# Parity tiles for the dilated attention, four strips for the modulation sums, and two slots weighed alone

## The reference

```python
A_PATTERNS = ((128, 1), (512, 4), (2048, 16))        # window, dilation, one group of 8 heads each
def hybrid_layer(x, mod, ...):
    shift, scale, gate = split(mod)                  # mod = silu(c) @ w_ada + b_ada
    h = rms_norm(x, norm_g) * (1 + scale) + shift
    a_qkv, a_z, m_cq, m_ckv, m_kr, m_z, merge = split(h @ w_in)
    y_a = dilated_mixer(a_qkv, rel_bias) * silu(a_z)
    y_m = mla_mixer(...) * silu(m_z)                 # latent attention, 16 heads
    g_a, g_m = split(sigmoid(merge))
    return x + gate * ((g_a * (y_a @ w_out_a) + g_m * (y_m @ w_out_b)) @ w_o)
```

## Time and profile before

| | |
|---|---|
| median of 3 runs | 2422.16 us (2420.01 to 2424.64) |
| the profiled execution | 2423.71 us |
| its span | 2421.9 us |
| instructions | 28489 |
| PE busy | 1964.8 us (81%) |
| DVE, ACT, POOL busy | 56%, 29%, 25% |
| moved by DMA | 744.49 MB, mean 307 GB/s |

### The profile page before, as it was taken

The page is one execution under the profiler, slowest core; times in us unless marked ns, Lnnn a source line. Parts: engine busy times, 40 slices in busy tenths (PEclk is TensorE's granted clock), DMA queues, the critical chain, the costliest instruction groups (busy, mean ns, idle before and its releaser), DMA issues.

```text
span 2421.9 us, 28489 instructions
## 1 busy us (share of the span) xinstructions
PE 1964.8 (81%) x10561; PEld 1127.1 (47%) x10561; DVE 1357.4 (56%) x3340; ACT 713.2 (29%) x2013; POOL 610.5 (25%) x531
## 2 busy tenths in 40 slices
PE   8997878556867866877776656659999999999998
PEld 6654444111532421442431111115877884787786
DVE  5657856767777467687577876442433422004433
ACT  1222422333262323353333333220014320003430
POOL 0002433454334334334344444430000000000000
PEclk9998998777998887899887686789999999999999
DMA  8547999999999999999999999986752343532322
GB/s 302 212 127 299 401 406 416 419 421 421 419 419 406 415 418 416 419 418 410 419 418 418 406 422 417 414 363 229 282 195 62 105 140 110 206 134 78 132 99 83
DMA packets 199351, 744.49 MB, mean 307 GB/s; under 512 B 42326, under 2 KB 55662, under 8 KB 133672
## 3 DMA queue, kind: packets, MB, share of 16 engines
q0 software_dynamic: 73728, 536.90, 53.8%
q1 hardware_dynamic: 112500, 201.82, 23.5%
q10 hardware_dynamic: 12984, 3.94, 0.7%
HBM read 741.49 MB, written 1.12 MB: 307 GB/s over the span
## 4 chain that ended last, share of the span: by engine, by line
PE 42%; DMA 37%; DVE 9%; ACT 4%; issue 3%; PEld 3%; POOL 1%; PEldq 0%; DVEq 0%; SPq 0%; ACTq 0%; POOLq 0%
DMA expert_rows<-in_peer_uv,expert_ids 35%; PE psum L326 12%; PE psum L3387 6%; PE psum L2164 5%; DVE expert_rows L2264 4%; PE psum L2848 3%; PEld psum L3140 3%; PE psum L3403 2%; PE psum L1848 2%; ACT coefs_on_diagonal L2581 1%; PE psum L3212 1%; PE psum L3434 1%; PE psum L2013 1%; PE psum L3034 1%; PE psum L3421 1%
## 5 line engine op out<-in xcount | busy, mean ns | idle before, releaser
L2164 PE MATMUL psum<-expert_rows,coefs_on_diagonal 64*64 64x512 f32 x4096 | 682.6, 779 | 420.8 <-ACT coefs_on_diagonal L2581 420.4
L2264 DVE SCALAR_TENSOR_TENSOR expert_rows<-expert_rows,x 128x1024 f32<-128x1024 f32 x512 | 627.1, 1225 | 412.6 <-DMA expert_rows<-in_peer_uv,expert_ids 409.3
L2744 POOL DMA_INDIRECT expert_rows<-in_peer_uv,expert_ids x512 | 604.0, 1180 | 1001.8 <-PE psum L2164 752.5
L2164 PEld LDWEIGHTS psum<-expert_rows,coefs_on_diagonal 64*64 64x64 f32 x4096 | 149.2, 160 | 812.0 <-ACT coefs_on_diagonal L2581 602.7
L2571 ACT ACTIVATE gelu_dots<-dots 128x2 f32<-128x2 f32 x256 | 52.1, 204 | 881.8 <-DVE expert_rows L2264 881.6
L326 PE MATMUL psum<-xT,ring 128*128 128x256 f32 (+1 forms) x1264 | 277.9, 381 | 2.3 <-DMA ring<-in_mlstm_w_in 2.3
L326 PEld LDWEIGHTS psum<-xT,ring 128*128 128x128 f32 (+1 forms) x1264 | 238.0, 189 | 42.1 <-issue 9.8
L2581 ACT ACTIVATE coefs_on_diagonal<-ident,coefs 128x128 f32<-128x128 f32 x512 | 177.5, 393 | 8.3
L1848 PEld LDWEIGHTS psum<-xT,ring 128*128 128x128 f32 (+1 forms) x1088 | 129.3, 183 | 78.4 <-issue 78.4
L3059 POOL COPY ring<-ring 128x512 f32<-128x512 f32 x2 | 1.2, 614 | 587.9 <-DMA ring<-in_w_uq 587.9
L1848 PE MATMUL psum<-xT,ring 128*128 128x128 f32 (+1 forms) x1088 | 148.7, 287 | 0.0
(11 more groups left out here) (440 smaller groups left out, 2030.4 us busy)
## 6 DMA issues: line engine op xcount, KB each, us to landing
ring<-in_w_in SPq DMA_DIRECT2D x64, 1024.0 KB, 7.3
ring<-in_peer_w_q SPq DMA_DIRECT2D x24, 1024.0 KB, 19.0
first_modulation_weights<-in_w_ada SPq DMA_DIRECT2D x12, 1024.0 KB, 7.3
ring<-in_w_out SPq DMA_DIRECT2D x12, 1024.0 KB, 12.4
ring<-in_w_ada SPq DMA_DIRECT2D x12, 1024.0 KB, 6.5
expert_rows<-in_peer_uv,expert_ids POOLq DMA_INDIRECT x512, 16.3
ring<-in_rglru_w_in SPq DMA_DIRECT2D x8, 1024.0 KB, 21.1
ring<-in_w_out_b SPq DMA_DIRECT2D x8, 1024.0 KB, 6.3
```

Of the source, the lines that this page charges most:

```text
L2164: last = pe.matmul(psum[64 * half:64 * half + 64, 2 * t + m, :], diag[tokens, n % DIAGS, tokens], rows[tokens, at_, D + half * 512:D + (ha ...
L2264: dve.scalar_tensor_tensor(out=rows[:, at_, 0:D], in0=rows[:, at_, 0:D], scalar=1.0, in1=x[:, n // TILE % NT, :], op0=ALU.mult, op1=ALU.mu ...
L2744: pool_.indirect_dma_start(out=rows[:, n % ROWS, :], out_offset=None, in_=table, in_offset=bass.IndirectOffsetOnAxis(ap=ids[:, at_:at_ + 1 ...
```

## The change

- Queries and the keys of groups 1 and 2 (dilations 4 and 16) are written to the chip with even tokens first and odd tokens behind (`copy_parity`); the keys of group 0 stay in token order. A query tile is now the even or the odd tokens. It sees all 256 keys of group 0 and the 128 keys of its own parity in groups 1 and 2: 512 columns a head for both tiles.
- The values of groups 1 and 2 are dealt to even and odd by four transfers from chip memory to chip memory (64 partitions x 4 KB each), which ACT issues behind the reading of `rc`; PE waits for them ahead of the first `weighted`.
- The bias tiles are loaded in six transfers, in pieces of 512 bytes, and issued behind the loads of `rc`, ahead of those of `rmz`.
- Scores have two banks a head, used in turn, so that they wait for the maxima of the step before the last; the transposes have one bank a head, the attention's output bank 6; `shared` is gone.
- `Modulation` reduces by four products into four strips of 32 partitions, DVE adds four times 128.
- The last two slots of the stream are weighed singly, and the hold of the second block's first loads is given up after slot 505 in place of slot 508.

```diff
-            for half in range(2):
-                if n >= RING:
+            if n >= RING:
+                for half in range(2):
                     pe.wait_ge(bank_read[n % RING][half].sem, n // RING)
-                pe.matmul(bank(n % RING, half)[0:1, 0:256], ones[:, 0:1], self.acc[:, g % 2, half * 256:half * 256 + 256],
-                          start=True, stop=True).then_inc(half_done[half].sem, 1)
+            for part in range(4):
+                last = pe.matmul(self.sums(n, part), ones[:, 0:1], self.acc[:, g % 2, part * P:(part + 1) * P],
+                                 start=True, stop=True)
...
+        def sums(self, n, part):
+            return bank(n % RING, part // 2)[32 * part:32 * part + 1, 0:P]
...
+        def tiles_in(col, offset, step):
+            src = bass.AP(scr.tensor, offset, [[step, P], [DA_G * SPAN, DA_H], [1, P]])
+            sp.dma_start(bias[:, :, col:col + P], src).then_inc(skew_sem.sem, 16)
...
+                elif n == slots - 1:
+                    pe.wait_ge(coefs.sem, c0 + slots // PAIR + 1)
...
-                weigh(p)
+                if n < slots - PAIR:
+                    weigh(n, PAIR)
+                else:
+                    weigh(n, 1)
+                    weigh(n + 1, 1)
...
-        weights.hold = (added.sem, ad0 + slots - 3)
+        weights.hold = (added.sem, ad0 + slots - 6)
...
-        if layer == 0:
-            weights.small_loads = keep.pop("bias_rows")
         rz = weights.add([(w, 0, P, KD)], 4608, 512, 1)
...
         rc = weights.add([(w, 0, P, KD)], 5120, 416, 1)
+        if layer == 0:
+            weights.small_loads = keep.pop("bias_rows")
         rmz = weights.add([(w, 0, P, KD)], 5536, 512, 1)
...
+        def copy_parity(copy, dst, b):
+            return copy(dst.rearrange("p a (e i) -> p a e i", e=2), b.rearrange("p (a i e) -> p a e i", a=2, e=2))
...
+            for c in range(NT):
+                for e in range(2):
+                    act.dma_start(dealt[64 * c:64 * c + 64, e, :], vt[e:P:2, c, DA_W:DA_G * DA_W])\
+                        .then_inc(values_dealt.sem, 16)
             s1(act)
...
-        fill = (0, 2, 3, 4, 5, 6, 7, 1)
+        fill = (0, 1, 2, 3, 4, 5, 7, 6)
...
+            own = slice(t * P, (t + 1) * P)
+            return [(0, 0, slice(0, T)), (1, T, own), (2, T + P, own)] if t == 0 else [(1, 0, own), (2, P, own), (0, T, slice(0, T))]
...
+            first = 2 * i + step % 2 if dilated else 2 * i
+            return psum[:, first, 0:width(tile_of(step))]
...
+            return psum[:, 4 + (i if dilated else 2 * i), 0:width(tile_of(step))]
+        out = psum[:, 6, 0:T] if dilated else psum[:, 1, 256:512]
+        spare = 1 if dilated else 0
...
-                if step:
-                    pe.wait_ge(biased.sem, b0 + step)
+                if step > spare:
+                    pe.wait_ge(biased.sem, b0 + step - spare)
...
+                elif values_at:
+                    pe.wait_ge(*values_at)
```

More of the change, by code:

```diff
@@ L2577, in weigh @@
                 if s >= DIAGS:
-                    act.wait_ge(added.sem, ad0 + s + PAIR - DIAGS)
-                for q in range(PAIR):
+                    act.wait_ge(added.sem, ad0 + s + count - DIAGS)
+                for q in range(count):
                     ins = act.activation(diag[:, (s + q) % DIAGS, :], ident[:, :], ACT.Copy,
@@ L2811, in second_layer @@
         if layer == 0:
-            place[0] = ya_end + 8 * 1024
+            place[0] = ya_end + 2 * 1024
             mod = Modulation(1)
+            assert place[0] <= at_phase + 72 * 1024
             place[0] = attend_at
@@ L2896, in scalar @@
             read_both(act, rz, lambda g, half, b: act.activation(az[:, 2 * half:2 * half + 2, :], two(b), ACT.Silu))
-            for run, dst, first in rqk:
-                read_out(act, 0, run, lambda g, b: act.copy(dst[:, first:first + 2, :], two(b)))
+            for i, (run, dst, first) in enumerate(rqk):
+                read_out(act, 0, run, lambda g, b: copy_parity(act.copy, dst[:, first:first + 2, :], b) if dealt_in(i)
+                         else act.copy(dst[:, first:first + 2, :], two(b)))
             if mod:
@@ L2901, in scalar @@
             read_both(act, rc, lambda g, t, b: act.copy(lat[:, t, :], b[:, 0:416]))
+            n = rv_.first + rv_.count - 1
+            for half in range(2):
+                act.wait_ge(bank_read[n % RING][half].sem, n // RING + 1)
+            for c in range(NT):
+                for e in range(2):
+                    act.dma_start(dealt[64 * c:64 * c + 64, e, :], vt[e:P:2, c, DA_W:DA_G * DA_W])\
+                        .then_inc(values_dealt.sem, 16)
             s1(act)
@@ L2969, in bias_of, with da_value @@
         def bias_of(p, t):
-            both = [by_group(bias[:, 2 * p + i, :])[:, :, 0:(t + 1) * P] for i in range(2)]
-            return [b[:, :, ::-1] for b in both]
+            return [bias[:, 2 * p + i, t * T:t * T + 512].rearrange("p (b k) -> p b k", b=4)[:, :, ::-1] for i in range(2)]
+        def da_value(p, i, g, c):
+            first = (2 * p + i) * DA_D
+            if g:
+                return dealt[:, c, (g - 1) * DA_W + first:(g - 1) * DA_W + first + DA_D]
+            return vt[:, c, first:first + DA_D]
         rmz_last = weights.add([(w, 0, P, KD)], 6048, 512, 1)
@@ L3314, in second_layer, with pair_attention @@
             stage(tensor=tensor, vector=vector, scalar=scalar)
-    def pair_attention(n, queries, keys, values, groups, scale, bias_of, z, y, beside=(), then=None):
+    def pair_attention(n, queries, keys, values, groups, scale, bias_of, z, y, beside=(), then=None, values_at=None):
         steps, G = 2 * n, groups
@@ L3414, in turn @@
                 flat = probs[t][i].rearrange("p g k -> p (g k)")
-                blocks = list(range(G * (t + 1)))
-                shared = blocks[:2] if len(blocks) > 4 and i else []
-                for b in [b for b in blocks if b not in shared] + shared:
-                    if shared and b == shared[0]:
-                        pe.wait_ge(copied.sem, c0 + 2 * step + 1)
-                    last = pe.transpose(bank_t(step, i)[:, b * P:(b + 1) * P], flat[:, b * P:(b + 1) * P], ident[:, :])
+                for b in range(width(t) // P):
+                    at_ = home(t, b)
+                    last = pe.transpose(bank_t(step, i)[:, at_ * P:(at_ + 1) * P], flat[:, b * P:(b + 1) * P], ident[:, :])
                 last.then_inc(turned.sem, 1)
```

112 lines of the change are left out of this document (70 added, 42 removed).

## The result

The changed kernel takes 2406.1 us (median of five runs, 2401.8 to 2410.8), the kernel before 2422.2 (five runs beside them, 2418.6 to 2425.0). The ratio is 0.9940, with a 95% interval of 0.9928 to 0.9953, which is 11.4 to 17.4 us less. The forecast was 2406.0. The profiled execution took 2410.8 us, the longest of the five, and has a span of 2409.0. Three executions far above the others of their kernel (3196.8 and 5026.5 us of the variant attention_alone, 3207.8 of the kernel before) are left out of every median and ratio given here.

The account below looks back on a forecast made before the run. PE's timeline was taken to bound the kernel (PE 42% of the span, DMA 37%). Terms -11.3 + 0 + 0 - 3.0 - 1.45 = -15.8 us gave 2406 from a median of 2422.2, range 2403 to 2409.

Parts of the forecast that it names:

- Attention: Dilated attention, two layers: fewer score columns, transposes and waits save 5.55 us in layer 0 and 5.75 in layer 1, -11.3.
- rival C: Stream's end and layer 1's attention: gathers don't suffer (-2.4) and the low clock goes (-1.7); total -19.9, 2402 us; 12%.
- Dealing: Values dealt by four ACT transfers: 2.5 us of issues fit the room and the 1 MB is hidden; 0, bound +2.
- Bias tiles: Bias loads between `rc` and `rmz`: 10.7 us at 28 ns a piece, `rmz` 3.3 us ahead of need; 0.
- Rival D: Late `rmz`: 512 B bias pieces cost as much as 1 KB ones; +4, 2410 us; 8%.
- E: Slower than before: bias pieces cost as 2 KB ones, PE stands 18.6 us for `rmz`; total +2.8, 2425 us; 4%.
- Strips: Modulation sums: four strips take 0.40 us in place of 1.02, six times, one saving lost, DVE's additions hidden; -3.0.
- The stream's end: Last slots and first loads: single weighing and earlier hold release, slots stretched to 3.24 us, first product at 1630.6; -1.45.
- Rival A: Stream's end: gathers keep only half the slow engine, a slot takes 4.96 us; +4.6 there, total -9.7, 2412 us; 10%.

Follow-up runs that it names:

- attention_alone: Changed kernel with modulation sums, pairs of slots and hold as before; attention, dealing and bias tiles kept: 2409.8 us, ratio 0.9949.
- wait_back: Changed kernel with the removed wait put back: the second head's turns wait after two blocks for ACT's copy of the first head: 2410.1 us.
- bias_twice: Changed kernel with the six bias tile loads made twice, the second set behind the landing of the first, ahead of `rmz`: 2423.8 us.
- bias_twice_deal_late: As bias_twice, but the four dealt transfers are issued behind ACT's reading of `rmz`: 2421.1 us.
- warm_hold4: As warm, but the hold on the second block's first loads is given up after slot 507 in place of 505: 2405.0 us, ratio 0.9923.
- bias_first: Changed kernel with DVE adding the bias of a sum ahead of its multiplication for the next sum: 2405.6 us, ratio 0.9929.
- hold_late: Changed kernel with the hold given up after slot 508, the last two slots still weighed singly: 2411.1 us.
- warm: bias_first plus three needless PE products ahead of each of the last groups of slots, over the last 16 slots: 2404.9 us, ratio 0.9934.

## Why the prediction was right, and where its steps were not

The time was met (2406.1 against 2406.0), with one term too small, one too large, and one half eaten by the clock. That it was met to a tenth is luck: the five runs lie 9 us apart, and the errors of the terms partly cancel.

- **Attention, -11.3 forecast, -12.5 measured.** Layer 0 came as worked out: -5.4 against -5.55. Scores 1.15 forecast and measured; a pair 13.25 and 13.24; the two last weighted products 3.0 us forecast, 1858.66 - 1855.45 = 3.2 measured. The weighted product took 1.89 where 1.93 to 1.96 was put. wait_back shows the wait that was forecast: 0.68 a pair and 2.7 a layer hung on it. Layer 1 gave 1.3 more than its term, because the low clock of its last product went; the prediction had left it in, with its going as -1.7 of rival C. It is gone in all twelve profiles with the new attention; what made it go isn't shown, as layer 0's product had the same gaps ahead of it and ran at the full clock.
- **Dealing, 0 forecast, 0 measured.** The four issues took 2.48 us (2.5 forecast). The stretch up to the attention is 16.43 us in both kernels. But the step said of the 1 MB only that it had time, not that it cost others any: bias_twice and bias_twice_deal_late show 6.2 us of the engines' time taken from the weights when these are late.
- **Bias tiles, 0 forecast, 0 measured.** 293 GB/s were measured, and 28 ns a piece give the same. The room was smaller than the 3.3 us forecast: in warm_hold4, where everything ahead is 1 to 2 us shorter and SP issues `rmz` at 1771.53, PE waits 0.21 us for it at 1784.32, 12.8 us behind the issue. With the same 12.8 us the changed kernel's `rmz`, issued at 1775.72, would be there at 1788.5, 1.7 us ahead of need, an estimate. The forecast had SP issue at once; SP took 11.08 us to issue the six transfers of bias tiles and came to `rmz` only then. Rival D (+4) and E (slower) didn't come. The Trainium skill, "DMA: Bandwidth & Descriptors", "Specifications", names 512 B as the least that still goes at the line's rate; here 293 GB/s stand against 387 with 2 KB pieces, so at 512 B the rate was a quarter lower. The bias tiles' pieces also start at skewed addresses, a few bytes further for each partition, and no run separates this from their size.
- **Strips, -3.0 forecast, -1.5 measured. This is the step that failed.** The sentence "DVE's four additions in place of two are hidden" is wrong. DVE adds the bias of a sum behind its multiplication for the next, and that addition gives back the bank that PE's next product needs. With shorter sums PE is there sooner, and the additions take 1.18 us for four in place of 0.74 for two: PE waits 0.8 us in three places. Also the wait on the load of `w_ada`, which the forecast charged at 0.7, grew by 1.2. bias_first removes the first and is 2.84 below before, 2.3 to 2.8 below the three profiles with the old sums.
- **The stream's end, -1.45 forecast, -2.2 measured at the first product, -0.5 at the transposes of tile 1.** The shared slot was put at 3.24 us; the dots came 3.11 and 3.27 apart. Rival A (4.96 us a slot) is refuted. But the prediction misread the rule that it named. The Trainium skill, "DMA: Bandwidth & Descriptors", "Queues, rings and completion order", says that an engine goes round the queues packet by packet; it doesn't say that the turns are equally long. The trace of before shows turns equal in number: from 300 to 330 us, where the weight queue moved 1338 pieces in 23.5% of the time, the gathers' queue has this row:

```profile
q0 software_dynamic: 1338, 9.74, 78.5%
```

Both queues moved as many pieces, one of at most 8 KB for each one of 2 KB, so the time goes by the size of the pieces. It also prices the slot: its 128 rows are eight on each of sixteen engines, and eight turns of 85 ns for the weights add 0.68 us to 2.48, 3.16 by this estimate. The product began 0.8 us ahead of forecast. The forecast had the hold given up at -0.3 from the dot of slot 507 and 3.6 slots stretched, 2.7 us in all; PE made slot 505 at the low clock (3.69 us for the pair, not 1.95), SP issued only at +1.55, and two slots were stretched, by 1.4 us together. What the step didn't ask is at which clock that product would run. In before's profile it ran at full speed; in attention_alone, with the same end of the stream, it did not; of the ten profiles with the new attention and without needless products, six have 15.4 to 15.7 us from the first product to the transposes, two have 14.8 and 15.3, and two 13.8. So before's profile was at the good end. Against profiles whose first product was as slow, the transposes come 2.2 us sooner (attention_alone) and 1.1 sooner (hold_late).

By its own rivals: the price of C's attention half (-1.7) came, its other half (gathers undisturbed) did not. The terms' errors, -1.2 on the attention, +1.5 on the strips and +0.95 at the stream's end, partly cancel, to -14.5, and the stretches of the two profiles say -14.4. That the medians moved by 16.1 is within their interval; the stream's drift of 1.5 us between the profiles is of the size of what is left.

## What to carry to other kernels

A shorter instruction on the critical engine is worth its saving only if the engine that hands it its next bank keeps up: follow the bank's release back through the other engine's program order, and put the step that releases ahead of the one that doesn't. A wait inside a repeated loop is worth finding: 0.68 us in each of eight pairs was a third of this change's gain. When loads are let in early, look at what they are mixed with: moving their start by 5 us, or slowing the gathers by them, changed 0.1 us, while a further 4 us, with the engines nearly idle before them, cost 1.2.

No version here beats the changed kernel beyond doubt. By its stretches warm is 3.0 us shorter (1.6 at the stream's end, 1.4 at the sums); by their medians bias_first, warm and warm_hold4 (2405.6, 2404.9, 2405.0) and the changed kernel (2406.1) are not told apart.

## What the runs showed of the hardware that was not expected

- Dealing 1 MB from chip memory to chip memory in pieces of 4 KB costs the sixteen DMA engines 5.2 to 6.6 us (14.0% of a window of 37 us in the changed kernel, 29.8% of one of 22 us in bias_twice), where 1 MB of weights takes 2.7 us at 387 GB/s. So a byte dealt from every other partition to others is about twice as dear there as one from DRAM (1.9 to 2.4 times).
- PE's clock fell in the stream's last slots and in the first product behind it, or didn't, in kernels with the same code there; the 32 instructions took 13.97 to 15.86 us (wait_back). Needless products between the slots kept the granted clock at 1.00 there. Why some kernels kept it without them is open.
- Two queues at work on the same engines moved 1338 pieces each in 30 us, one of 2 KB for one of a gathered row, so the time was shared 23.5% to 78.5%. Weight loads that run beside gathers so slow these by 0.63 to 0.86 us a slot, though the engines had seemed nearly idle (a share of 0.08); why one engine lags so far behind the others at the end of the stream wasn't tried.
